# Two attentions that finish one head before they start the other

## The reference

```python
z = einsum(qb, kb) * scale                    # keys 0 .. q0 + 127
log_fail = where(strict, log_sigmoid(-z), 0)
after = cumsum(log_fail, reverse=True) - log_fail
w = where(strict, exp(log_sigmoid(z) + after), 0)
out = w @ vb
```

## Time and profile before

| | |
|---|---|
| median of 3 runs | 3518.51 us (3518.41 to 3521.21) |
| the profiled execution | 3525.73 us |
| its span, from the first to the last instruction | 3524.0 us |
| PE busy | 3086.6 us, 88% of the span |
| DVE busy | 1644.3 us, 47% |
| ACT busy | 1060.8 us, 30% |
| POOL busy | 315.6 us, 9% |
| mean granted TensorE clock | 0.928 of full speed |

### The profile page before, as it was taken

The page is one execution under the profiler, slowest core; times in us unless marked ns, Lnnn a source line. Parts: engine busy times, 40 slices in busy tenths (PEclk is TensorE's granted clock), DMA queues, the critical chain, the costliest instruction groups (busy, mean ns, idle before and its releaser), DMA issues.

```text
span 3524.0 us, 38000 instructions
## 1 busy us (share of the span) xinstructions
PE 3086.6 (88%) x15115; PEld 2529.0 (72%) x15115; DVE 1644.3 (47%) x2095; ACT 1060.8 (30%) x1521; POOL 315.6 (9%) x349
## 2 busy tenths in 40 slices
PE   4889999999676887999999976988769699999997
PEld 3667778778564675888888855876647588888885
DVE  3445465564673445333332353443453554554545
ACT  3441441531612343111111133444453321221222
POOL 0110110210200000000000000322330000000000
PEclk8999999999886997999999997988879799999998
DMA  2331222222102342112111123233314311111112
GB/s 85 84 96 40 82 89 63 74 66 72 56 1 104 117 135 98 42 42 65 36 48 59 36 90 105 61 110 110 104 73 149 102 48 42 60 42 42 60 42 89
DMA packets 216339, 256.95 MB, mean 73 GB/s; under 512 B 10366, under 2 KB 174476, under 8 KB 216220
## 3 DMA queue, kind: packets, MB, share of 16 engines
q1 hardware_dynamic: 191776, 173.58, 15.8%
q0 software_dynamic: 12464, 44.34, 3.7%
q10 hardware_dynamic: 11980, 37.41, 3.5%
HBM read 197.05 MB, written 58.25 MB: 72 GB/s over the span
## 4 chain that ended last, share of the span: by engine, by line
PE 78%; DVE 10%; ACT 4%; issue 3%; DMA 3%; ACTq 1%; POOL 0%; DVEq 0%
PE PS L319 30%; PE PS L342 17%; PE PS L556 17%; PE PS L1268 2%; DVE h_gained L399 1%; PE PS L1234 1%; PE PS L1174 1%; PE PS L2235 1%; PE PS L2224 1%; ACT hH L408 1%; DVE hL L413 1%; PE PS L1163 1%; PE PS L1327 1%; ACTq L471 1%; PE PS L2266 1%
## 5 line engine op out<-in xcount | busy, mean ns | idle before, releaser
L319 PE MATMUL PS<-hH,w_H 128*128 128x512 f32 x1408 | 436.7, 391 | 15.3 <-DVE hL L413 15.3
L319 PE MATMUL PS<-hL,w_H 128*128 128x512 f32 x1408 | 435.4, 391 | 0.0
L319 PE MATMUL PS<-hH,w_L 128*128 128x512 f32 x1408 | 434.8, 390 | 0.0
L556 PE MATMUL PS<-hH,w_H 128*128 128x512 f32 x1008 | 422.6, 419 | 11.6 <-DVE w_L L304 6.4
L556 PE MATMUL PS<-hH,w_L 128*128 128x512 f32 x1008 | 401.0, 398 | 0.0
L556 PE MATMUL PS<-hL,w_H 128*128 128x512 f32 x1008 | 400.1, 397 | 0.0
L304 DVE TENSOR_TENSOR w_L<-w_raw,w_H 128x1024 fp32r<-128x1024 f32 x192 | 234.6, 1223 | 351.6 <-ACT w_H L299 350.2
L1747 DVE TENSOR_TENSOR ffn_sum<-ffn_sum,PS 128x1024 f32<-128x1024 f32 x176 | 214.8, 1220 | 300.2 <-PE PS L342 300.2
L319 PEld LDWEIGHTS PS<-hH,w_H 128*128 128x128 f32 x1408 | 264.6, 189 | 72.6 <-DVE hL L413 16.1
L319 PEld LDWEIGHTS PS<-hL,w_H 128*128 128x128 f32 x1408 | 265.5, 189 | 55.7
L319 PEld LDWEIGHTS PS<-hH,w_L 128*128 128x128 f32 x1408 | 265.3, 188 | 55.6
(11 more groups left out here) (363 smaller groups left out, 4570.8 us busy)
## 6 DMA issues: line engine op xcount, KB each, us to landing
w_raw<-in_w_in SPq DMA_DIRECT2D x63, 512.0 KB, 4.3
w_raw<-in_w_up SPq DMA_DIRECT2D x44, 512.0 KB, 3.9
u_scratch<-unit_staged SPq DMA_DIRECT2D x42, 512.5 KB, 4.8
w_raw<-in_w_ffn_gate SPq DMA_DIRECT2D x22, 512.0 KB, 3.8
w_raw<-in_w_ffn_up SPq DMA_DIRECT2D x22, 512.0 KB, 3.8
down_raw<-in_w_ffn_down SPq DMA_DIRECT2D x11, 1024.0 KB, 4.9
down_raw<-in_w_down SPq DMA_DIRECT2D x11, 1024.0 KB, 5.1
u_scratch<-unit_staged_f SPq DMA_DIRECT2D x21, 512.0 KB, 4.4
```

Source lines behind the costliest of these rows:

```text
L319: mm = e.matmul(PS[:, bank + half, :], w[:, k, :], x[:, k - x0, half * HALF:(half + 1) * HALF], start=(i == 0 and j == 0), stop=(i == len( ...
L556: mm = e.matmul(PS[:, half, :], w[:, k, :], x[:, k, half * HALF:(half + 1) * HALF], start=(k == 0 and j == 0), stop=(k == KT - 1 and j == 2))
```

## The change

The list `ATT` is turned: all 8 row blocks of head 0, then all 8 of head 1. The widths of the 16 steps become 1, 2, 3, up to 8, and then once more 1 to 8. Since all engines read the same list, the numbers and the sizes of their instructions stay as they were in sum, and only their order changes.

The two heads of a row block now lie 8 steps apart, so the output is put together head by head. `o_sum` is chosen by `s % 2`. `o_out` is called for each step and handles 64 partitions, so it runs 16 times for each pair and no longer 8 times. It has a new wait on `weights_written` for POOL's own last `weigh`, and after each call within the loop POOL waits for its own `o_att_taken`. `o_add(s)` waits for `o_out(s-2)`. The stage F part of the diff is alike; its lines for `weights_written` and the first store are shown.

```diff
-        ATT = [(h, r) for r in range(NB) for h in range(2)]
+        ATT = [(h, r) for h in range(2) for r in range(NB)]
...
-                def o_out(r):
-                    e.wait_ge(sem("att_o_summed"), at(2 * r + 2, p, NA))
-                    e.tensor_tensor(o_rows[:, r * P:(r + 1) * P], o_sum[r % 2][:, 0:P],
-                                    o_sum[r % 2][:, P:2 * P], ALU.add).then_inc(sem("o_att_taken"), 1)
+                def o_out(s):
+                    h, r = ATT[s]
+                    e.wait_ge(sem("weights_written"), at(min(s + 3, NA), p, NA))
+                    hs = slice(h * HD, (h + 1) * HD)
+                    e.wait_ge(sem("att_o_summed"), at(s + 1, p, NA))
+                    e.tensor_tensor(o_rows[hs, r * P:(r + 1) * P], o_sum[s % 2][hs, 0:P],
+                                    o_sum[s % 2][hs, P:2 * P], ALU.add).then_inc(sem("o_att_taken"), 1)
 
                 for s in range(NA):
                     weigh(s)
-                    if s % 2 and s >= 3:
-                        o_out(s // 2 - 1)
-                o_out(NB - 1)
-                e.wait_ge(sem("o_att_taken"), at(NB, p, NB))
+                    if s >= 2:
+                        o_out(s - 2)
+                        e.wait_ge(sem("o_att_taken"), at(s - 1, p, NA))
+                o_out(NA - 2)
+                o_out(NA - 1)
+                e.wait_ge(sem("o_att_taken"), at(NA, p, NA))
...
                 def o_add(s):
                     h, r = ATT[s]
                     e.wait_ge(sem("att_o_upper"), at(s + 1, p, NA))
-                    if r >= 2:
-                        e.wait_ge(sem("o_att_taken"), at(r - 1, p, NB))
-                    e.tensor_tensor(o_sum[r % 2][h * HD:(h + 1) * HD, :], PS[0:HD, o_bank(s), 0:2 * P], o_up[s % 2][:, :],
+                    if s >= 2:
+                        e.wait_ge(sem("o_att_taken"), at(s - 1, p, NA))
+                    e.tensor_tensor(o_sum[s % 2][h * HD:(h + 1) * HD, :], PS[0:HD, o_bank(s), 0:2 * P], o_up[s % 2][:, :],
                                     ALU.add).then_inc(sem("att_o_summed"), 1)
...
+                    e.wait_ge(sem("weights_written"), at(min(s + 4, NA), pp, NA))
...
+                    if s == 0 and p:
                         e.wait_ge(sem("o_att_stored"), 16 * pp)
```

More of the change, by code:

```diff
@@ L1950, in weigh, with o_out @@
                         .then_inc(sem("weights_written"), 1)
-                def o_out(r):
-                    e.wait_ge(sem("att_o_summed"), at(2 * r + 2, pp, NA))
-                    if r == 0 and p:
+                def o_out(s):
+                    h, r = ATT[s]
+                    e.wait_ge(sem("weights_written"), at(min(s + 4, NA), pp, NA))
+                    hs = slice(h * HD, (h + 1) * HD)
+                    e.wait_ge(sem("att_o_summed"), at(s + 1, pp, NA))
+                    if s == 0 and p:
                         e.wait_ge(sem("o_att_stored"), 16 * pp)
-                    e.tensor_tensor(o_rows_F[:, r * P:(r + 1) * P], o_sum_F[r % 2][:, 0:P],
-                                    o_sum_F[r % 2][:, P:2 * P], ALU.add).then_inc(sem("o_att_taken"), 1)
+                    e.tensor_tensor(o_rows_F[hs, r * P:(r + 1) * P], o_sum_F[s % 2][hs, 0:P],
+                                    o_sum_F[s % 2][hs, P:2 * P], ALU.add).then_inc(sem("o_att_taken"), 1)
                 weigh(0)
@@ L1962, in pool_F @@
                         weigh(s + 1)
[L1963 to L1966, removed]
+                    if s >= 2:
+                        o_out(s - 2)
+                        e.wait_ge(sem("o_att_taken"), at(s - 1, pp, NA))
+                o_out(NA - 2)
+                o_out(NA - 1)
+                e.wait_ge(sem("o_att_taken"), at(NA, pp, NA))
                 e.dma_start(o_scr[p], o_rows_F[:, :]).then_inc(sem("o_att_stored"), 16)
@@ L2136, in o_add @@
                     e.wait_ge(sem("att_o_upper"), at(s + 1, pp, NA))
-                    if r >= 2:
-                        e.wait_ge(sem("o_att_taken"), at(r - 1, pp, NB))
-                    e.tensor_tensor(o_sum_F[r % 2][h * HD:(h + 1) * HD, :], PS[0:HD, o_bank(s), 0:2 * P],
+                    if s >= 2:
+                        e.wait_ge(sem("o_att_taken"), at(s - 1, pp, NA))
+                    e.tensor_tensor(o_sum_F[s % 2][h * HD:(h + 1) * HD, :], PS[0:HD, o_bank(s), 0:2 * P],
                                     o_up_F[s % 2][:, :], ALU.add).then_inc(sem("att_o_summed"), 1)
```

## The result

The changed kernel took 3539.9 us (median of 5 runs, 3532.84 to 3542.22), the kernel before 3519.0 beside it (5 runs, 3518.41 to 3522.78). The ratio is 1.0054, 95% interval [1.0039, 1.0069]: slower by more than the 0.2% that such a measurement can tell, and outside the predicted range of 3516 to 3534.

A forecast was written before the change was run, and what follows sets the result against it. PE was taken to bound the kernel, with losses mainly in the two last pairs without filler. Terms 3.0 + 1.8 + 0 + 0 + 0.8 = 5.6 us on 3518.5 gave 3524.1 us, range 3516 to 3534.

The forecast's parts named there:

- Stage B, pair 3: Last pair of stage B, without filler: even and odd steps carry unequal widths, so loops wait: +1.8 us (0 to 2.8).
- the loads: DMA issues holding ACT's queue in step 8, stage B pair 3: no difference, 0 us (-2.8 to +0.5).
- Starts: Start of each attention, stages B and F: wider first steps delay PE's first weights, +3.0 us (0 to 6).
- filled pairs: Stage B pairs with filler: new head-change stalls against old stalls saved, 0 us (-2.2 to +4.4).
- thinner cover: Rival: wide steps in stage B's filled pairs 1 and 2 stall PE, 8.5 us more, 3532.6 us; chance 0.28.
- wait of `o_add` for POOL: Sign: DVE's `o_add` should not be seen waiting for POOL's `o_out`; stall priced at 0 in stage B.
- POOL in stage F, pair 3: Last pair of stage F: POOL nearly binds, and added `o_out` and waits lengthen its path: +0.8 us.
- Colliding `o_out`: Rival: in stage F, pair 3, each added `o_out` takes 1.93 us instead of 0.46: 3535.9 us; chance 0.03.
- POOL in stage B: Stage B, all four pairs: the added `o_out` and waits fit into POOL's idle time, no stall, 0 us.

The follow-up runs named there:

- e17: Kernel before with one more POOL memset of some 0.45 us ahead of each weighing in stage B's last pair: 3524.4 us, ratio 1.0018.
- e4: Changed kernel plus 16 dummy matmuls that keep PE busy behind the attention of stage B's last pair: 3531.0 us, 1.0028 against the kernel before.
- e9: New order in stage B's last pair alone, with 8 output additions there as before, new output steps elsewhere: 3524.4 us, 1.0002 against the kernel before.
- e3: Changed kernel with the old order of steps put back everywhere, new output steps kept: 3521.6 us, 0.9998 against the kernel before.
- Up and down: Stage B's last pair alone with one head in widths 1 to 8, the other 8 to 1: 3520.1 us; with 16 dummy matmuls 3519.2.
- e7: New order in the last pair of stage B alone, new output steps everywhere: 3532.9 us, 1.0034 against the kernel before.
- e1: New order in stage B alone, old order in stage F, new output steps everywhere: 3531.1 us, 1.0023 against the kernel before.
- e10: New order in stage B's last pair alone, its six DMA issues behind step 12 instead of 8: 3528.9 us, 1.0011 against the kernel before.
- e14: Changed kernel with the last stage B pair's DMA issues behind step 12 and 16 dummy matmuls: 3531.1 us, 1.0016 against the kernel before.
- e8: New order in the first three pairs of stage B, old order in its last: 3522.0 us, 1.0002 against the kernel before.
- e2: New order in stage F alone, old order in stage B, new output steps everywhere: 3529.3 us, 1.0022 against the kernel before.
- e13: New order in the first three pairs of stage F alone: 3523.5 us, 1.0008 against the kernel before.

## Why the prediction was wrong

**The last stretch of stage B splits into three terms.** With the clock high, the old order takes 235.8 to 237.0 us in six profiles (e17 aside), 236.5 in the mean, and the new order 240.1 and 240.4 (e4, e9): the order, with the loads in step 8, costs 3.7. With the clock low, the old order takes 245.4 (e3) and the new one 248.1 to 249.9 (five profiles, 249.4 in the mean): 8.9 and 9.2 more than with it high. The late loads take 2.8 to 3.1 off the latter (246.6, 246.3). Up and down shows the same clock term, 244.2 against 235.1. POOL's last output addition of the pair cuts the stretch more sharply. Behind it lie 126.8 to 127.9 us in the eleven profiles with the high clock and 135.1 to 136.1 in the nine with the low one, nothing between: 8.3 us by the means, whatever the order. Up to it the old order takes 109.1 us in the mean, the new one 113.5, and with the loads late 110.7 and 111.1. So the 13.4 us are some 4 to 5 of order and loads and some 8 to 9 of clock.

**The failed step: what follows the last pair.** My sum priced each pair up to its end and took everything behind it as unchanged. That PE's clock in the rwkv products is a state that some executions have high and some low was nowhere in it, nor was it a rival. It was to be seen in part: in the trace before, the clock falls to 0.57 between 968 and 980 us and climbs back just ahead of those matmuls. The new order had it low in 7 profiles of 9, two of the seven with dummies; the old order (e17 included) had it low in 1 of 8. The timed runs say likewise: without dummies all seven of e7 lay in the upper group, against 43 of 147 before. Going from 3 in 10 to all is worth 0.7 x 9 = 6 us in the mean, and in the median the full 9. The order doesn't do it alone, as the twelve runs of e9 show, and e1, with e7's order in that pair, had four of eleven runs some 5 us below the rest. What in the new order and its output steps keeps the clock low stays open. So does the rest of the 20.9 us: 7.7 by the medians belong to stage F, of which more below.

**Stage B, pair 3: +1.8 predicted (0 to 2.8), together with the loads 0 (-2.8 to +0.5).** The loop grew by 4.8. The loads were the mis-sized term: with the queue's share of 2.4 moved, 2.3 (e10) and 2.1 (e14) remain for the order in the loop, and 1.8 up to the last output addition: the 1.8 predicted, and inside its bounds. I had taken no difference, arguing that step 7, the widest, runs just ahead. The chain of the kernel after, in order of time, shows why that isn't so: ACT's queue is on the chain from 938.91 until ACT can fetch `o_upper` at 941.23, in the middle of narrow steps.

```profile
938.91 0.39 ACTq L724
...
939.33 0.49 ACTq L726
...
939.86 0.61 ACTq L727
...
940.50 0.62 ACTq L728
...
941.23 0.39 ACT o_upper L756
```

The old order had the same hold on its chain, but in front of widths 5 and 6, and there it cost less.

**Starts and filled pairs: 3.0 and 0 predicted; small, as predicted, but not measured.** From the start to the last pair of stage B the profiles of kernels with the new order there were 1 us longer in the mean than the others, with a scatter of 2 (0.9 predicted for three pairs); e8 had 1.5 by the medians of its chip and a ratio of 1.0002. A term of 1 us can't be told from such scatter. PE's wait at the value products outside pair 3 is 24.2 - 18.9 = 5.3 us, 4.4 before. Waits of PE over the span, and then in 901.5 to 968.6:

```profile
PE PS L1179 <- DVE weights_turned L908: 24.2, 18, 3.6
```

```profile
PE PS L1179 <- DVE weights_turned L908: 18.9, 12, 3.6
```

So the thinner cover, my rival with 0.28, is refuted in stage B: its stalls in the filled pairs aren't there (the sign set for it was over 6 us), though its time of 3532.6 lay nearer to the result. In the filled pairs of stage F that wait is 1.0 us before and after. No wait of `o_add` for POOL appeared.

**POOL in stage F, pair 3: as predicted.** Its loop takes 2611.55 - 2572.26 = 39.3 us, 38.7 before, so +0.6 where I had +0.8; no run leaves out the added operations there, so that POOL's path makes the 0.6 is argued, not shown. The timeline of POOL shows the predicted picture, hardly any idle time between widths 5 and 8:

```profile
2580.15 1.89 POOL L1954 TENSOR_SCALAR prob<-prob,den_inverse 128x640 f32<-128x640 f32 x1 [0.17 <-DVE den_inverse L2135]
2582.12 0.45 POOL L1964 TENSOR_TENSOR o_att_f<-o_sum_f 64x128 f32<-64x128 f32 x1
2583.09 2.21 POOL L1954 TENSOR_SCALAR prob<-prob,den_inverse 128x768 f32<-128x768 f32 x1 [0.51 <-DVE den_inverse L2135]
...
2586.02 2.53 POOL L1954 TENSOR_SCALAR prob<-prob,den_inverse 128x896 f32<-128x896 f32 x1 [0.19 <-DVE den_inverse L2135]
```

**Stage F as a whole stays open.** By its profile it costs the changed kernel 0.7 us, by the medians of e2 nearly 8. The profiles of e2 and e13, with the old order in stage B and the new one in F's filled pairs, have 2.9 and 2.6 us there; those that have the new order in both stages have at most 0.6. From F's last pair into stage G the profiles scatter over 6 us in either order; the six with the new order there are 2.3 us longer in the mean than the thirteen with the old one. The runs don't settle what of this is order and what is clock.

**Colliding `o_out`: where I had it, none; where I had nothing, many, and nearly harmless to the loop.** Single lines: shortest, median and longest in ns, for stage B and stage F after, and for the old order with the new output steps.

```profile
L645 POOL TENSOR_TENSOR o_att<-o_sum x64: 447/458/2417, 131.7 to 968.1; 64x128 f32<-64x128 f32 x64
```

```profile
L1964 POOL TENSOR_TENSOR o_att_f<-o_sum_f x64: 447/455/467, 2227.3 to 2620.6; 64x128 f32<-64x128 f32 x64
```

```profile
L645 POOL TENSOR_TENSOR o_att<-o_sum x64: 448/460/2527, 130.8 to 962.8; 64x128 f32<-64x128 f32 x64
```

At least 13 of the 64 in stage B took over 1 us, 4 of them in the last pair. Yet the old order with 7 long ones in its last pair has a loop of 50.7 us, no longer than before: there the cover holds, as I had said of POOL in stage B. Whether these long additions have a part in the low clock, which left when half of them went (e9), is not tested.

## What to carry to other kernels

Where a stretch has no filler, put DMA issues of a computing engine's queue in front of wide steps: the same six cost 2.4 us more in front of narrow ones. When a change touches a thin stretch, look also at the dense PE work right behind it and at the granted clock there: that the time before varies between runs in two groups some 9 us apart is the warning, and a change can move most runs into the upper one. Compare profiles by landmarks that both kernels issue, and compare several profiles before a difference is put down to the change. Compare a remedy with its control on the same chip: the share of upper runs of one and the same kernel went from 1 in 21 to 18 in 35. None of the orders tried beat the old one by more than the measurement tells; the kernel before with 16 dummy matmuls came out at 0.9987 [0.9976, 0.9998], so at most a little faster, by losing its upper group.

## What the hardware showed that I had not expected

PE stayed at 1.2 GHz through matmuls that kept it busy without a gap, in nine profiles, while others had it at 2.4 GHz for the same instructions at nearly the same place. Going by the two groups of the timed runs, it seems that one and the same kernel has now the one and now the other; I can't say from which detail of the stretch ahead. In the old order sixteen dummy matmuls there made the upper group rarer, 0 of 12 runs against 10 of 26 on one chip; in the new order the clock was low behind them in two of three profiles.

In stage B an output addition of POOL that starts while a DVE scan runs ends with the scan: all 14 that took over 0.9 us after the change, and the 16 of e3, ended 0.23 to 0.26 us behind one. A scan can be held by POOL likewise. Timelines of POOL and of DVE, kernel after: the addition of 0.45 us took 2.42 beside a scan that ended at 931.65, and the scan of width 1, 0.42 us at its shortest, took 1.31 until the weighing had ended at 933.97.

```profile
929.47 2.42 POOL L645 TENSOR_TENSOR o_att<-o_sum 64x128 f32<-64x128 f32 x1
931.97 2.00 POOL L637 TENSOR_TENSOR stick_kept<-stick_kept,stick_left 128x1024 f32<-128x1024 f32 x1
```

```profile
929.36 2.29 DVE L902 TENSOR_TENSOR_SCAN stick_left<-stick_left,zero_column 128x1024 f32<-128x1024 f32 x1 [0.82 <-ACT stick_left L740]
...
932.94 1.31 DVE L902 TENSOR_TENSOR_SCAN stick_left<-stick_left,zero_column 128x128 f32<-128x128 f32 x1
```

In stage F, where DVE's long operations read PSUM, none of 64 additions took over 467 ns. The Trainium skill, GPSIMD Engine Reference, Key points, names such contention for DVE instructions with two SBUF inputs; both stages agree with it, by 30 long additions in stage B and none in stage F.
